# A list scheduler in the kernel's builder sets the order of the instructions, the PSUM banks and the SBUF places of a hybrid attention trunk

## The reference

```python
h = rms_norm(x, g_in)
(c_q, c_kv, k_pe, z_mla, q_swa, k_swa, v_swa, z_swa, q_mem, z_mem) = split_cols(h @ w_in, IN_SIZES)
y_mla = mla_attention(c_q, c_kv, k_pe, g_q, g_kv, w_uq, w_ukv, cos, sin) * jax.nn.silu(z_mla)
y_swa = swa_attention(q_swa, k_swa, v_swa, sinks, rel_table) * jax.nn.silu(z_swa)
y_mem = memory_attention(q_mem, rms_norm(mem, g_mem), w_mem_kv) * jax.nn.silu(z_mem)
y = jnp.concatenate([y_mla, y_swa, y_mem], axis=-1) @ w_out
return x + y          # then one more rms_norm outside
```

## Time and profile before

| | us |
|---|---|
| median of 3 runs (lowest, highest) | 1190.93 (1189.53, 1206.58) |
| the profiled execution | 1191.29 |
| span of its slowest core, core 3 | 1189.7 |
| spans of cores 0 to 7 | 1100.5, 1178.8, 1069.7, 1189.7, 1093.3, 1179.0, 1067.8, 1180.1 |
| busy on core 3: PE, PEld, DVE, ACT, POOL | 772.5, 336.1, 552.1, 401.6, 22.9 |
| moved by DMA on core 3 | 89.03 MB |

### The profile page before, as it was taken

One profiled execution on the slowest core, in us unless ns is written; L12 is line 12 of the kernel. 1 busy time (PEld: TensorE's weight loads), 2 busy tenths in 40 slices (PEclk: granted clock), 3 DMA queues, 4 the chain that ended last, 5 costly groups with the idle time before them and its releaser, 6 DMA issues.

```text
span 1189.7 us, 11158 instructions; the slowest of 8 cores (1067.8 to 1189.7 us)
## 1 busy us (share of the span) xinstructions
PE 772.5 (65%) x3697; PEld 336.1 (28%) x3697; DVE 552.1 (46%) x730; ACT 401.6 (34%) x533; POOL 22.9 (2%) x61
## 2 busy tenths in 40 slices
PE   0614265685573567585585768877777787756995
PEld 0202132342231123242232423442232332222442
DVE  1314435434335444445456556675465665531333
ACT  0202401005202453432432345635445565430212
POOL 2000000000000000000000000000000000000000
PEclk9867677987796577797787889988798999787998
DMA  6960633431530034432134000000000025065421
GB/s 136 234 152 18 141 106 107 142 106 36 142 117 7 0 66 136 93 113 71 35 118 90 1 0 1 2 1 1 1 1 1 1 34 108 1 218 119 159 106 74
DMA packets 15178, 89.03 MB, mean 75 GB/s; under 512 B 1644, under 2 KB 1776, under 8 KB 7928
## 3 DMA queue, kind: packets, MB, share of 16 engines
q1 hardware_dynamic: 9528, 57.65, 13.7%
q0 software_dynamic: 5568, 30.41, 12.9%
HBM read 106.40 MB, written 7.34 MB: 96 GB/s over the span
## 4 chain that ended last, share of the span: by engine, by line
PE 39%; DVE 27%; ACT 16%; issue 9%; DMA 8%; DVEq 1%; POOL 0%; ACTq 0%; POOLq 0%; SPq 0%
PE psd L335 39%; ACT pmb_r L315 4%; ACT sq_r L315 4%; DVE w_r L318 4%; DVE p_r L318 4%; ACT ze_r L315 2%; DVE sq_r L318 2%; DMA ws_r<-wkv 2%; DMA wo_r<-wo 2%; DVE acc_r L318 2%; DMA self_r<-sel 2%; DVE z_r L318 2%; DVE qv_r L318 2%; DVE sw_r L322 1%; ACT rin_r L315 1%
## 5 line engine op out<-in xcount | busy, mean ns | idle before, releaser
L335 PE MATMUL psd<-x_r,w_r 128*128 128x512 bf16 (+1 forms) x896 | 218.9, 410 | 150.8 <-DVE w_r L318 150.8
L315 ACT ACTIVATE pmb_r<-psd 128x768 bf16<-128x768 f32 (+2 forms) x188 | 158.3, 904 | 114.2 <-PE psd L335 35.5
L335 PEld LDWEIGHTS psd<-x_r,w_r 128*128 128x128 bf16 x896 | 96.3, 110 | 271.6 <-issue 219.1
L335 PE MATMUL psd<-Qn_r,K_r 128*128 128x384 bf16 (+2 forms) x392 | 110.1, 368 | 30.3 <-ACT pmb_r L315 25.2
L335 PE MATMUL psd<-pmb_r,V_r 128*128 128x384 bf16 (+2 forms) x392 | 94.9, 369 | 20.1 <-DVE oc_r L329 19.7
L335 PE MATMUL psd<-x_r,wkv_r 128*128 128x512 bf16 (+4 forms) x432 | 83.3, 373 | 31.9 <-DVE wkv_r L1232 30.2
L318 DVE TENSOR_TENSOR p_r<-pmb_r,pmb_r 128x768 bf16<-128x768 bf16 (+1 forms) x88 | 54.4, 619 | 105.5 <-ACT pmb_r L315 74.5
L318 DVE TENSOR_TENSOR w_r<-st_r,gv_r 128x1024 bf16<-128x1024 f32 x72 | 87.2, 1216 | 0.0
L335 PE MATMUL psd<-wo_r,gA_r 128*128 128x512 bf16 x224 | 56.9, 400 | 20.3 <-DMA wo_r<-wo 20.3
L315 ACT ACTIVATE ze_r<-z_r 128x512 f32<-128x512 f32 (+1 forms) x32 | 18.5, 578 | 152.3 <-DVE z_r L318 128.0
L335 PE MATMUL psd<-Qp_r,kpe_r 64*128 64x384 bf16 (+2 forms) x392 | 59.3, 369 | 11.1 <-ACT pmb_r L315 6.1
(11 more groups left out here) (117 smaller groups left out, 827.7 us busy)
## 6 DMA issues: line engine op xcount, KB each, us to landing
st_r<-wti SPq DMA_DIRECT2D x28, 1024.0 KB, 4.9
st_r<-wmk SPq DMA_DIRECT2D x8, 1024.0 KB, 5.7
x_r<-xu POOLq DMA_DIRECT2D x8, 1024.0 KB, 10.5
wo_r<-wo POOLq DMA_DIRECT2D x4, 2048.0 KB, 20.4
xo_r<-xo SPq DMA_DIRECT2D x7, 1024.0 KB, 9.1
out<-xo_r SPq DMA_DIRECT2D x14, 512.0 KB, 2.6
ws_r<-wkv POOLq DMA_DIRECT2D x4, 1024.0 KB, 20.0
x_r<-xu POOLq DMA_DIRECT2D x4, 768.0 KB, 43.8
```

The lines of the kernel that those rows point to most:

```text
L315: self.P.op("act", lambda e: e.activation(out=out, in_=in_, func=func, **kw), reads, writes, 0.19 + n / 1200.0)
L335: ins = e.matmul(out, lhsT=l, rhs=r, start=s0, stop=s1, skip_group_check=True)
```

## The change

No operation is added or removed. `Prog.op` now only notes the operation with a cost in microseconds that the builder assumes (`glue` marks every second `front`, which must follow the one before it on PE). `graph` links operations that read and write the same parts, `schedule` then plays all engines against these assumed costs and gives out the order, `layout` places the buffers by that order, and `finish` works out the semaphores. The rules of `schedule` are: of all ready operations the one that can start first is taken, among those within 0.05 us of it on its engine the one recorded first; DMAs of a queue keep their recorded order; PE may take an operation up to 16 PE operations ahead of its first one still open; the other engines up to 140 recorded operations ahead of it; a bank or pair of banks is given to an operation when it starts, from all eight (the attention's output no longer has banks of its own); SBUF in use is held under a limit, tried from 200 KB downwards until `layout` fits.

```diff
-    def op(self, eng, fn, reads=(), writes=(), cost=0.0, what=""):
-        self.i += 1
-        self._touch(list(reads) + list(writes))
-        wl = self._waits(eng, reads, writes)
...
+    def op(self, eng, fn, reads=(), writes=(), cost=0.0, what="", glue=False, prio=0):
+        o = Op()
+        o.i = len(self.all)
+        o.eng = {eng: (fn, cost)} if isinstance(eng, str) else eng
...
+    def schedule(self, limit, pewin, look):
+        self.graph()
+        n = len(self.all)
+        free = {e: 8.0 for e in self.ENG}
...
+            pelim = pes[min(pehead + pewin, len(pes) - 1)].i
+            mark = pes[pehead].i if pehead < len(pes) else n
...
+                for o in ready[e]:
+                    if o.mb is not None:
+                        if fifo[e][0] is not o or o.i > mark + look:
+                            continue
+                    elif e == "pe":
+                        if o.i > pelim or (glued is not None and o is not glued):
+                            continue
+                    elif o.i > mark + look:
+                        continue
+                    s = max(free[e], o.est[e])
+                    add = sum(b.size for b in o.bufs if b.first is None)
+                    if add:
+                        lim = limit - (0 if o.i <= head else 16384 if o.mb is not None else 4096 if o.i < mark + 40 else 8192)
+                        s = room(add, s, lim)
+                        if s is None:
+                            continue
...
+                smin = min(c[0] for c in cand)
+                s, o = min((c for c in cand if c[0] <= smin + 0.05), key=lambda c: c[1].prio)
+                fin = s + o.eng[e][1]
+                if best is None or (s, fin) < best[0]:
+                    best = ((s, fin), e, o)
...
+            if o.mb is not None:
+                t = max(fin + 1.2, dmafree)
+                dmafree = t + o.mb * 3.1
+                o.end = dmafree + 1.2
+                fifo[e].pop(0)
...
-        self.obank = None
-        for b in (6, 7):
-            self.free.remove(b)
...
-        self.mm(lst, rd, [self.PS[k], self.PS[k + 1]], "front")
+        self.mm(lst, rd, [self.PS[k], self.PS[k + 1]], "front", flip)
...
+        if st["first"]:
+            self.ob[p, bq] = self.ps2()
+        ob = self.ob[p, bq]
...
-                lst.append((self.pf(6 + h, c0, c0 + w), V[:, tile, h * 128:h * 128 + 128], pb[:, h, o:o + w],
+                lst.append((self.pf(ob + h, c0, c0 + w), V[:, tile, h * 128:h * 128 + 128], pb[:, h, o:o + w],
...
-        for final in (False, True):
-            P = Prog(nc, sems, plan, "r%d" % role)
-            Role(P, role, dr, DB).run()
-            if not final:
-                plan, top = P.layout(SBMAX - SB0)
-                PLANS.append((role, top))
+        for limit in (200, 194, 188, 182, 176, 170):
+            P = Prog(nc, sems, None, "r%d" % role, DB)
+            Role(P, role, dr).run()
+            plan = P.schedule(limit * KB, 16, 140)
+            if P.layout(plan, SBMAX - SB0):
+                break
...
+        P = Prog(nc, sems, plan, "r%d" % role, DB)
+        Role(P, role, dr).run()
+        P.finish()
```

More of the change, by code:

```diff
@@ L69, with bisect_in @@
 STUB = Stub()
+def bisect_in(l, x):
+    k = len(l)
+    while k and l[k - 1] > x:
+        k -= 1
+    l.insert(k, x)
 class Buf:
-    __slots__ = ("t", "size", "first", "last", "off", "parts", "init", "name")
+    __slots__ = ("t", "size", "first", "last", "off", "parts", "init", "name", "left")
 class Part:
-    __slots__ = ("buf", "w", "r", "ps", "rq")
+    __slots__ = ("buf", "w", "r", "bank", "rq", "lw", "lr", "old")
+class Op:
+    __slots__ = ("i", "eng", "fn", "cost", "reads", "writes", "glue", "mb", "out", "what", "succ", "npred", "est", "prio",
+                 "start", "end", "pos", "banks", "bufs")
 class Prog:
@@ L91, in __init__ @@
         self.tag = tag
-        self.ops = {e: [] for e in self.ENG}
-        self.cnt = {e: 0 for e in self.CE}
-        self.known = {e: {} for e in self.ENG}
+        self.DB = DB
+        self.all = []
         self.bufs = []
[L96 to L100, removed]
+        self.banks = []
     def buf(self, name, shape, dtype):
@@ L133, in new @@
         return b.t, self.part(b)
[L135 to L150, removed]
-                                        d[k] = max(d.get(k, 0), v)
-                    b.init = tuple(list(d.items()) for d in ev)
-                for q in b.parts:
-                    q.w, q.r = list(b.init[0]), list(b.init[1])
-            b.last = self.i
@@ L157, in _waits, with bank @@
-    def _waits(self, eng, reads, writes, skip=None):
-        need = {}
-        def add(ev):
-            k, v = ev
-            if k != skip and v > need.get(k, 0):
-                need[k] = v
-        for b in reads:
-            for ev in b.w:
-                add(ev)
-            if b.ps and b.rq is not None and b.rq != eng:
-                for ev in b.r:
-                    add(ev)
-        for b in writes:
-            for ev in b.w:
-                if ev[0] != eng or eng == "pool" or b.ps:
-                    add(ev)
-            for ev in b.r:
-                add(ev)
+    def bank(self, n):
+        v = len(self.banks)
+        if n == 2 and v % 2:
+            self.banks.append(None)
+            v += 1
+        for i in range(n):
+            self.banks.append([self.part(None, v + i), n, v])
+        return v
@@ L176, in _waits, with add @@
+    def _waits(self, eng, reads, writes):
+        need = {}
+        def add(l):
+            for k, v in l:
+                if v > need.get(k, 0):
+                    need[k] = v
+        for p in reads:
+            add(p.w)
+            if p.bank is not None and p.rq is not None and p.rq != eng:
+                add(p.r)
+        for p in writes:
+            add(x for x in p.w if x[0] != eng or eng == "pool" or p.bank is not None or p.old)
+            add(p.r)
         kn = self.known[eng]
@@ L236, in replay, with __init__, __getitem__ @@
                 handle.wait_ge(self.semof(k), v)
[L238 to L265 removed]
+class Banks:
+    def __init__(self, P):
+        self.P = P
+    def __getitem__(self, v):
+        return self.P.bpart(v)
 class Role:
[L271 removed]
+    def __init__(self, P, role, dr):
         self.P = P
```

404 lines of the change are left out of this document (308 added, 96 removed).

## The result

The changed kernel takes 844.11 us (median of 3 runs, 843.12 to 846.88) against 1190.93 before: ratio 0.7097, 95% interval 0.7057 to 0.7137. The profiled execution has a span of 845.3 us on its slowest core. Executions of any of these kernels in which one die ran at a lower granted clock and ended some per cent later are left out of every ratio, and of the times under "The experiments".

A forecast was written before the change was run, and what follows sets the result against it. The prediction took waits between engines on core 3, mainly PE's for `w_r` behind DVE's order, as the bound, with a floor of 655 us of PE work. Seven terms summed to -247: 1191.3 to 944 us, range 860 to 1070.

The forecast's parts named there:

- Term 6: Whole kernel: denser PE runs more at the upper clock level, matmuls get faster; -45 us, ends -90 and 0.
- My cross-check: Whole kernel: 655 us of work at a clock of 0.92 is 712 busy, leaving 172 idle, 18% of the span.
- Term 1: Projections: weight folds ahead of result copies on DVE remove PE's waits for `w_r`; -130 us, ends -162 and -60.
- Term 7: Weight tile pairs: their transfers take longer than their matmuls; +10 us, ends 0 and +35.
- Term 3: Projections: other waits, for attention results that DVE takes out late, shrink; -15 us, ends -29 and 0.
- Term 4: Attention: fewer waits for `pmb_r` and `oc_r`, but scores may bunch; -35 us, ends -65 and +20.
- Terms 2 and 5: Start: `sq_r` wait goes, first matmul later, net -12 us; output: last weight blocks asked for earlier, -20 us.
- Folds wait for transfers: DVE's queue: folds run ahead of late transfers and hold up copies and PE; 1064 us, chance 0.14.
- Slower: DVE's queue: folds standing before their tiles land stop every copy, PE's banks fill; 1264 us, chance 0.06.
- The order doesn't reach the end: Whole kernel: a core gains nothing or a wait moves; 1191 us, chance 0.03.
- Nearly all idle goes: Projections and attention: waits for `w_r`, other projection waits and attention idle at their near ends; 868 us, chance 0.12.
- Clock limited: All cores denser at once: busy stretches stay at about the 0.828 clock, +79 us; 1023 us, chance 0.10.

The follow-up runs named there:

- a_only_dve: Changed kernel with PE, ACT and POOL held to the recorded order, DVE free, 56 KB left free by transfers: 934.5 us, 0.789 of the kernel before.
- a_room: Changed kernel with 56 KB of memory left free by transfers in place of 16, no engine held: 858.2 us, 0.723 of the kernel before.
- a_fifo: Changed kernel with PE, DVE, ACT and POOL each held to the recorded order, 56 KB left free by transfers: 1110.8 us, 0.938 of the kernel before.
- b_obank: Kernel before with the attention's output in any free pair of banks in place of 6 and 7: 1178.5 us, 0.992.
- a_late_w: Changed kernel with small constants loaded first, bias table and first three weight tiles later, 24 KB left free: 841.1 us, 0.708 of the kernel before.
- b_fold_ahead: Kernel before with one more weight tile folded before its turn: 1114.5 us, 0.937.

## Why the prediction was too high

The direction and the mechanism were right; the sizes of terms 6, 1, 4 and 7 were not, all to the same side. Term by term on core 3, from 1189.7:

| term | forecast | measured |
|---|---|---|
| 1, waits for `w_r` | -130 | -162 |
| 2, start | -12 | -9 |
| 3, other waits of the projections | -15 | -23 |
| 4, attention | -35 | -57 |
| 5, weights of the output | -20 | -20 |
| 6, clock | -45 | -98 |
| 7, transfers | +10 | 0 |
| sum | -247 | -370 |

**Term 6 failed by the most**: -45 forecast, -98 measured, 53 of the 123 us. I gave back half of the loss in the `w_r` matmuls and a third elsewhere. The rows held the better rule: busy time and gaps go together. With the clock at 0.76 to 0.79 in stretches that were 40% idle and 1.00 in the output, removing nearly all gaps brings nearly all of it back: 674.1 us busy against my floor of 655. The floor itself took the output's 87.9 us at the full clock, where rows 3 grant 0.93; by the rule used for the other stretches it is 649. My cross-check took a clock of 0.92; core 3's is 0.973.

**Term 1**: I left 1 us for each of 32 waits as a matter of caution, with no row for it, and none is left. `a_only_dve` shows that the order of DVE's queue is the cause. **Term 7**, +10, was not there: weights land in 6.6 us from 130 to 290 us (4.9 before), and no wait of PE or DVE for them reaches the path, since they are asked for earlier: the only waits of DVE for `st_r` are two at the start, 6.1 and 3.5 us. With `a_room`, which asks later, 14 us come back, 9 of them on core 3, where waits for `w_r` of 10.6 us are in the view again.

**Term 3**, -23, lies in its range, but its working was wrong: it took the 36.2 us wait out of the idle time of 98 to 692 us, and that wait ended at 98.69:

```profile
98.69 0.80 PE L335 MATMUL psd<-sq_r,ones_r 128*128 128x384 bf16 x2 [36.16 <-DVE sq_r L318]
```

Only 0.7 us of it lie in that stretch, so the other waits there were 64 us and not 29, and the near end of -29 had no ground.

**Term 4**: only the waits for `oc_r` and part of `pmb_r` were seen as removable. `a_fifo` shows that without any new order on a compute engine 45 of the 57 us go, by banks and places as far as the waits tell; the one line on banks that I costed, the free pair for `oc_r`, gives 4 us on core 3 in `b_obank` (medians). The fear that the scores would bunch was wrong: waits for `pmb_r` fell from 31.3 to 21.9.

**Terms 2 and 5** held, term 2 partly by luck. The first matmul came at 61.0, forecast 55: the transfers as worked out (`self_r` used at 54.4, forecast 53), and then 4.7 us of constants on DVE ahead of the first cast. The measured -9 is +33.6 for the start and -42.7 for `sq_r`, where I had +24 and -36: two errors that nearly cancel. And 24 of 28 us is too much to count as loss: in `a_late_w` a first matmul 22.2 us earlier brings core 3's end forward by 4 to 10 us.

**The slowest core.** I forecast core 3 and took the rest to follow. Core 3 ends 123 us below the sum, and core 0, 26 us above it, is what the median shows. Folding ahead had nothing to give there (`b_fold_ahead`), but other waits of its own went with the new order, 99 to 168 us by DVE's alone: before, 65.5 us for `sq_r`, 35.1 for `pw_r`, 34.9 for `wuq_r`, 26.9 for `z_r`. Now:

```profile
PE psd L596 <- DVE wkv_r L1491: 40.5, 3, 34.8
PE psd L596 <- ACT pmb_r L576: 31.7, 34, 1.5
PE psd L596 <- DMA x_r<-xu: 14.7, 1, 14.7
```

**The rivals.** "Folds wait for transfers", "Slower" and "The order doesn't reach the end" are out: 370 us went on core 3, and DVE waits for `st_r` only at the start. "Nearly all idle goes" (868, given 0.12) was the right case, and too high itself, because it left term 6 at -45: gaps and clock move together. With term 6 at its near end of -90 as well, it gives 868 - 45 = 823, beside the 819.4 of core 3; that this is so close is partly luck, since it still holds term 7's +10. "Clock limited" is refuted for the profiled execution by core 3's mean clock of 0.973 and by the rows of one die, 720 to 760 us of the changed kernel, cores 0, 1 and 3:

```profile
720.00:760.00 40.00, 40.00 (x187) 18.16 (x186) 16.02 (x21) 10.17 (x32) 0.00 (x0) 1.00 0.47 168
720.00:760.00 40.00, 39.12 (x269) 22.12 (x267) 25.64 (x36) 19.75 (x30) 0.40 (x2) 1.00 0.10 25
720.00:760.00 40.00, 40.00 (x187) 18.17 (x186) 15.39 (x21) 9.89 (x30) 0.00 (x0) 1.00 0.36 123
```

Three cores of the die are 98 to 100% busy at a granted clock of 1.00. The Trainium skill (TensorE: Matmul & The Clock Gate, "Seeing it yourself") says that a die goes to 13/16 of the clock within about 5 to 20 us of a third core starting dense matmuls. This trace does not agree, 1.00 over 40 us, and the measurement decides for this kernel and its data. The page calls the limit dependent on the data, which no run here varies.

## What to carry to other kernels

Where an engine's granted clock is low beside its own gaps, price a gap at more than its length: in this kernel each microsecond of idle time that went took 0.36 us of matmul time along. Before a new order is judged, hold one engine at a time to the old order: it told in four runs that one queue carried most of the gain, and that banks, places and the moments of the loads carried a part that no wait by name had shown. Hold the loads too, which was left out here. And when one core's waits go, look at the next core's before you name the time.

## What the runs showed of the hardware

- At the start the transfers of core 3 land late: 1 MB in 24.8 us (median of six) within the first 130 us, 6.6 later; a 2 KB load issued behind 4.2 MB on SP's queue served its reader 33.4 us after its issue.
- A clock of 1.00 was granted on three cores of a die at once, 98 to 100% busy for 40 us.
- On core 3 the same 3697 matmuls took 772.5 us beside 417.2 us of idle time at a mean granted clock of 0.828, and 674.1 us beside 145.3 at 0.973.
- 65 us of matmuls put into gaps of the kernel before were free: 0.998 of the time [0.994, 1.002].
